# The attention of the first block: normalising before the transpose, the value product with V as weights, and a tail of 128 rows

## The reference, cut to what matters

```python
logits = jnp.einsum('bthd,btkhd->bthk', q_b, k_sel).astype(jnp.float32) * (HEAD_DIM ** -0.5)
logits = jnp.where(valid[:, :, None, :], logits, -jnp.inf)
p = jax.nn.softmax(logits, axis=-1).astype(v_sel.dtype)
return jnp.einsum('bthk,btkhd->bthd', p, v_sel)
```

## Time and profile before

| | |
|---|---|
| median of 3 runs | 1720.37 us (1720.04 to 1726.73) |
| the profiled execution | 1720.61 us |
| its span, first to last instruction | 1718.5 us |
| mean granted clock of TensorE | 0.979 |
| PE, DVE, ACT, POOL busy | 1640.2, 882.7, 384.0, 922.4 us |
| the stage `gates`, 322 to 534 us | PE busy 206.07 of 212 us |

### The profile page before, as it was taken

How to read it: one execution, slowest core, us unless ns; L and a number is a source line. 1 busy time by engine, 2 the same in 40 slices (tenths; PEclk the granted TensorE clock), 3 DMA queues, 4 the chain that set the end, 5 groups by cost and what they waited for, 6 DMA issues and landing times.

```text
span 1718.5 us, 23461 instructions
## 1 busy us (share of the span) xinstructions
PE 1640.2 (95%) x7899; PEld 1329.3 (77%) x7899; DVE 882.7 (51%) x1223; ACT 384.0 (22%) x740; POOL 922.4 (54%) x529
## 2 busy tenths in 40 slices
PE   4999999999999999999999998899788999999998
PEld 3769999877777888888888886677556788888886
DVE  6157830232443365531441456888655674574475
ACT  4130110123332012110110122143462330121122
POOL 4545555543446666757666665534213566666653
PEclk9999999999999999999999998899789999999998
DMA  4323333222122433333323332222001233333222
GB/s 154 90 74 86 87 81 90 76 61 57 54 61 83 143 98 90 94 98 97 87 85 110 88 96 67 68 62 62 25 25 50 86 98 93 91 98 98 88 84 86
DMA packets 264290, 142.61 MB, mean 83 GB/s; under 512 B 6205, under 2 KB 261461, under 8 KB 264101
## 3 DMA queue, kind: packets, MB, share of 16 engines
q1 hardware_dynamic: 262021, 139.26, 27.9%
q10 hardware_dynamic: 2208, 2.49, 0.4%
HBM read 137.41 MB, written 4.19 MB: 82 GB/s over the span
## 4 chain that ended last, share of the span: by engine, by line
PE 85%; DVE 10%; ACT 3%; issue 2%; DMA 0%; DVEq 0%; ACTq 0%; SPq 0%
PE PJ L548 64%; PE PJ L546 11%; PE PJ L871 1%; PE PB L702 1%; PE PX L683 1%; DVE CT L1416 1%; PE PB L693 1%; PE PX L636 1%; PE PB L703 1%; DVE H L1574 1%; DVE XC L1651 1%; DVE L L1609 0%; PE PJ L608 0%; DVE small L1596 0%; PE PX L857 0%
## 5 line engine op out<-in xcount | busy, mean ns | idle before, releaser
L494 POOL TENSOR_SCALAR WH<-RAW 128x1024 fp32r<-128x1024 f32 (+1 forms) x257 | 290.6, 1131 | 749.8 <-DMA RAW<-in_w_in_dram 325.5
L496 POOL TENSOR_TENSOR WL<-RAW,WH 128x1024 fp32r<-128x1024 f32 (+1 forms) x257 | 630.4, 2453 | 21.4
L548 PE MATMUL PJ<-AH,WH 128*128 128x512 f32 x944 | 381.0, 404 | 5.8 <-issue 3.4
L548 PE MATMUL PJ<-AH,WL 128*128 128x512 f32 x944 | 373.6, 396 | 0.0
L548 PE MATMUL PJ<-AL,WH 128*128 128x512 f32 x944 | 372.4, 395 | 0.0
L548 PE MATMUL PJ<-BH,WH 128*128 128x512 f32 x752 | 304.3, 405 | 7.3 <-DVE BL L1544 6.4
L548 PE MATMUL PJ<-BH,WL 128*128 128x512 f32 x752 | 299.9, 399 | 0.0
L548 PE MATMUL PJ<-BL,WH 128*128 128x512 f32 x752 | 299.6, 398 | 0.1
L548 PEld LDWEIGHTS PJ<-AH,WH 128*128 128x128 f32 x944 | 177.8, 188 | 54.5 <-issue 10.2
L548 PEld LDWEIGHTS PJ<-AL,WH 128*128 128x128 f32 x944 | 177.8, 188 | 40.8
L548 PEld LDWEIGHTS PJ<-AH,WL 128*128 128x128 f32 x944 | 177.8, 188 | 40.5 <-issue 0.2
(11 more groups left out here) (305 smaller groups left out, 1792.8 us busy)
## 6 DMA issues: line engine op xcount, KB each, us to landing
RAW<-in_w_in_dram SPq DMA_DIRECT2D x89, 512.0 KB, 3.7
RAW<-in_w_ff_up_dram SPq DMA_DIRECT2D x44, 512.0 KB, 3.8
RAW<-in_w_gate_dram SPq DMA_DIRECT2D x22, 512.0 KB, 3.8
RAW<-in_w_up_dram SPq DMA_DIRECT2D x22, 512.0 KB, 3.8
RAW<-in_w_out_dram SPq DMA_DIRECT2D x16, 512.0 KB, 3.9
RAW<-in_w_down_dram SPq DMA_DIRECT2D x16, 512.0 KB, 4.1
RAW<-in_w_ff_down_dram SPq DMA_DIRECT2D x16, 512.0 KB, 4.1
RAW<-in_w_conv_out_dram SPq DMA_DIRECT2D x8, 512.0 KB, 4.1
```

The costliest lines, as they stand in the source:

```text
L494: nc.gpsimd.tensor_scalar(WH[:, slot, 0:kc], RAW[:, slot, 0:kc], 1.0, 1.0, ALU.mult, ALU.mult).then_inc(w_hi, 1)
L496: nc.gpsimd.tensor_tensor(WL[:, slot, 0:kc], RAW[:, slot, 0:kc], WH[:, slot, 0:kc].bitcast(F32), ALU.subtract).then_inc(w_ready, 1)
L548: last = mm(bank_of(name, i)[0:rows], w[:, w_at, k, 0:rows], a[:, k, :], start=st, stop=sp_)
```

## The change

Three things are changed, all in the attention of `gates`:

1. The probabilities are scaled by the reciprocal of their row before they are transposed. The scaling is a DVE instruction on LT in place (144 to 528 columns), right behind the reciprocal; PE's `turn_p` waits for it (`p_scaled`) in place of `exp_done`. The scaling of the value product into YS is gone.
2. In `pv` V is the stationary operand and PT moves. The result then has the head width on the partitions, as QT wants it: `turn_y`, its wait and the YS tile are gone, and ACT copies PB7 into QT one step earlier (it waits for `pv_done`).
3. The tail product has 128 rows: the rows behind the 16 are set to zero once, in V by POOL near the start and in PT by DVE ahead of the stage. Two waits of ACT for these are new.

PE's loop of two rounds is written out, so that its waits are on constants.

```diff
+            pool.memset(V[:, QB, :], 0.0).then_inc(v_padded, 1)
@@ PE
-                pe.wait_ge(exp_done, i * (2 * NU) + (r * NU + u + 1))
+                pe.wait_ge(p_scaled, g + 1)
...
-                for t in range(b + 1):
-                    mm(PB7[:, 0:P], PT[:, u % 2, t * P:(t + 1) * P], V[:, t, at], start=t == 0, stop=False)
-                mm(PB7[:, 0:P], PT[0:META, u % 2, 4 * P:5 * P], V[0:META, b + 1, at],
-                   start=False, stop=True).then_inc(pv_done, 1)
-
-            def turn_y(i, r, u):
-                pe.wait_ge(ys_ready, i * (2 * NU) + (r * NU + u + 2))
-                pe.wait_ge(y_ready, i * (2 * NU) + (r * NU + u + 1))
-                nc.tensor.transpose(TURNED_Y[:, 0:P], YS[:, u % 2], ident[:]).then_inc(y_turned, 1)
+                pe.wait_ge(pt_ready, g + 2)
+                pe.wait_ge(y_ready, g + 1)
+                for t in range(b + 2):
+                    at = t if t <= b else QB
+                    last = mm(PB7[:, 0:P], V[:, t, h * P:(h + 1) * P], PT[:, g % 2, at * P:(at + 1) * P], start=t == 0, stop=t == b + 1)
+                last.then_inc(pv_done, 1)
...
-            with pe.Fori(0, 2) as i:
-                for r in range(2):
-                    for half in range(12):
+            for half in range(2 * COUNT["gates"]):
...
@@ ACT
+            act.wait_ge(v_padded, 1)
+            act.wait_ge(p_padded, 1)
-                    if 0 <= s - 3 < NU:
-                        u = s - 3
-                        act.wait_ge(y_turned, i * NU + (u + 1))
+                    if 0 <= s - 2 < NU:
+                        u = s - 2
+                        act.wait_ge(pv_done, i * NU + (u + 1))
...
-                           TURNED_Y[:, 0:P], ACT.Copy).then_inc(y_ready, 1)
+                           PB7[:, 0:P], ACT.Copy).then_inc(y_ready, 1)
@@ DVE
+            nc.vector.memset(PT[:, :, QB * P:(QB + 1) * P], 0.0).then_inc(p_padded, 1)
...
                         nc.vector.reciprocal(RINV[:, u % 4:u % 4 + 1], RS[:, u % 2:u % 2 + 1]).then_inc(rinv_ready, 1)
-                    if 0 <= s - 2 < NU:
-                        u = s - 2
                         dve.wait_ge(rinv_ready, i * NU + (u + 1))
-                        dve.wait_ge(pv_done, i * NU + (u + 1))
-                        ts(YS[:, u % 2], PB7[:, 0:P], RINV[:, u % 4:u % 4 + 1], None, ALU.mult).then_inc(ys_ready, 1)
+                        p = LT[:, u % 2, 0:EXT[units[u][1]]]
+                        ts(p, p, RINV[:, u % 4:u % 4 + 1], None, ALU.mult).then_inc(p_scaled, 1)
```

More of the change, by code:

```diff
@@ L238, in two_blocks @@
         QS = place(rt3, "QS", [P, 2, P])
-        YS = place(rt3, "YS", [P, 2, P])
         rt4 = again(r_t, t0)
@@ L676, in _, with qk @@
             NU = len(units)
[L678 to L683, removed]
+            def qk(g):
+                h, b = g // QB, g % QB
+                pe.wait_ge(qs_ready, g + 1)
+                pe.wait_ge(logits_ready, g + 1)
+                last = mm(PX[:, 0, 0:min(EXT[b], BANK)], QS[:, g % 2], KT[:, h, 0:min(EXT[b], BANK)], start=True, stop=True)
@@ L684, in qk, with turn_p @@
                 if EXT[b] > BANK:
-                    last = mm(PX[:, 1, 0:EXT[b] - BANK], QS[:, u % 2], head[:, BANK:EXT[b]], start=True, stop=True)
+                    last = mm(PX[:, 1, 0:EXT[b] - BANK], QS[:, g % 2], KT[:, h, BANK:EXT[b]], start=True, stop=True)
                 last.then_inc(qk_done, 1)
-            def turn_p(i, r, u):
-                j, b = units[u]
-                pe.wait_ge(exp_done, i * (2 * NU) + (r * NU + u + 1))
-                pe.wait_ge(pt_ready, i * (2 * NU) + (r * NU + u + 1))
+            def turn_p(g):
+                b = g % QB
+                pe.wait_ge(p_scaled, g + 1)
+                pe.wait_ge(pt_ready, g + 1)
@@ new lines, in _ @@
+            base = LETGO["gates"]
+            for half in range(2 * COUNT["gates"]):
+                j, turn, step_ = half // 2, half // 12, half % 12
+                if half % 2 == 0:
+                    i = 2 * (j // 6)
+                    if j % 3 == 2:
+                        pe.wait_ge(freed["dve"], base["dve"] + j // 3 + 1)
+                    else:
+                        pe.wait_ge(freed["act"], 2 * i + (base["act"] + (0, 0, None, 1, 2)[j % 6] - (1 if j % 6 == 0 else 0)))
+                panel("gates", j, j, a_x, mix, ks=halves()[half % 2], owner="here")
+                if 0 <= step_ - 2 < NU:
+                    pv(turn * NU + step_ - 2)
+                if 0 <= step_ - 1 < NU:
+                    turn_p(turn * NU + step_ - 1)
+                if step_ < NU:
+                    qk(turn * NU + step_)
@@ L1263, in _ @@
             ts, tt, stt = nc.vector.tensor_scalar, nc.vector.tensor_tensor, nc.vector.scalar_tensor_tensor
-            for e, credit in ((freed["dve"], CREDIT), (logits_ready, 1), (ys_ready, 1)):
+            for e, credit in ((freed["dve"], CREDIT), (logits_ready, 1)):
                 dve.sem_inc(e, credit)
```

16 lines of the change are left out of this document (7 added, 9 removed).

## The result

| | before | after |
|---|---|---|
| median of the runs | 1720.26 us (1720.04 to 1726.73, 4 runs) | 1753.14 us (1743.39 to 1754.93, 4 runs) |
| profiled execution, its span | 1720.61, 1718.5 us | 1754.61, 1752.9 us |
| first attention stage ends at | 533.78 us | 563.78 us |

Slower: ratio 1.017, 95% interval 1.0125 to 1.0215. The last row of the table is a mark that I use from here on: the start of the matmul behind the one wait of 2.10 us that closes the stage in every kernel. Up to it nothing but the stage differs. Here it is before and after, in PE's timelines.

A forecast was written before the change was run, and what follows sets the result against it. PE was taken as the bound, busy 95% of the span. Per turn, -3.2 us of list and the stops gave +5.3, with the clock +8.3; four turns +33 on 1720.6 us gave 1754 us, range 1738 to 1765.

The forecast's parts named there:

- What leaves PE: PE's list loses the transposes of results (0.9 us a turn) and tail time (2.3): -3.2 us a turn.
- Unit 0: PE at `turn_p` waits for the scaling, queued on DVE behind convolution and multiply into U: a stop of 3.9 us.
- Unit 5: PE at `turn_p` waits for the scaling, held by POOL's second pass after the second convolution: a stop of 3.65 us.
- the pass ends 7.27 after T4: POOL's pass at unit 5 ends 0.4 us later, from 6.87, counted from the start of unit 4's `turn_p` (T4).
- Unit 6: Reciprocal stands behind the multiply of step 7; PE at `turn_p` stops 0.8 us.
- Unit 7: POOL's second pass just ahead of the scaling: a stop of 1.6 us or 0; half taken, 0.8 us.
- Unit 1: Scaling waits for POOL's pass; a stop of 0.2 us in place of 0.9, so -0.7 us a turn.
- The stops together: Stop terms of a turn at PE's `turn_p`: +3.9 - 0.7 + 3.65 + 0.8 + 0.8 us.
- The clock: Two stops of over 3.5 us a turn each bring a clock fall of 1.6 us: 3.0 us a turn, bounds 0 and 3.2.
- Rival A: The stops come but the clock stays: 1742 us; chance 0.22.
- Rival B: POOL's passes don't meet the waits on DVE in steps 0, 5 and 8: -1.25 us a turn, 1715.6 us; chance 0.06.
- Rival C: The rows of the tail don't matter, all else as forecast: 1763 us; chance 0.07.

The follow-up runs named there:

- e6_order_tail16: e1_order with the last pass of each value product taking 16 rows again in place of 128: 1718.96 us.
- e1_order: Changed kernel, DVE reordered: convolutions at the end of the turn before, reciprocal and scaling ahead of the multiply into U: 1709.24 us.
- e9_before_order: Kernel before, with DVE's order of e1_order and no scaling to move: 1716.57 us.
- e10_recip_only: Changed kernel with only reciprocal and scaling moved ahead of the multiply into U, convolutions where they were: 1741.65 us.
- e3_pool_small: Changed kernel with POOL's passes over the weights of panels 48 to 67 cut from 1024 columns to 128: 1723.36 us.
- e2_fill: Changed kernel with unused products put on PE ahead of its waits of units 0 and 5: 1744.65 us.
- e5_before_padded: Kernel before, with its tail alone padded from 16 rows to 128: 1713.49 us.
- e4_order_act: e1_order with the scaling done by ACT behind its exponential in place of DVE: 1702.89 us.
- e8_act_scale: Changed kernel in its own order, with the scaling alone moved from DVE to ACT: 1737.61 us.
- e7_conv_only: Changed kernel with only the convolutions moved to the end of the turn before, reciprocal and scaling where they were: 1724.99 us.

## Why the prediction was right

The forecast was 1754 us, the median is 1753.14. Its own terms, one by one:

- **What leaves PE, -12.8 us in four turns: right, a little small.** The tail was to give 9.3 and gives 10.9, with the 0.06 us of the transposes behind it (e6_order_tail16 against e1_order). Those of the results were to give 3.5 and give 3.7 (e9_before_order against e6_order_tail16). Together -14.6 us. But each of the stops takes a little more than its idle time, which had no term: without the stops, a turn of after is still 0.8 us longer than one of e1_order (16.04 us against 15.81 from unit 7 to the next unit 0, and 0.2 us each at units 5, 6 and 7).
- **Unit 0, 3.9 us:** measured 3.38, 3.82, 3.83 and 3.81. e10_recip_only shows the multiply's part (0.65), e3_pool_small what is left with short passes (1.5).
- **Unit 5, 3.65 us:** measured 2.90 to 3.03. The mechanism held, the term was 0.7 too large. The step that failed is "the pass ends 7.27 after T4": the pass did not move. It starts 4.16 us after T4 (415.57 less 411.41), where it started 4.17 after it in the kernel before. The traces show why. The load of the weights did shift by the 0.4 us: SP issues it 1.16 us ahead of T4 before and 0.77 after. But the weights land 0.1 us sooner, and POOL's pass over the high part, which takes 1.35 us before, takes 1.05 after:

```profile
400.13 0.38 SPq L405 DMA_DIRECT2D RAW<-in_w_in_dram  x1
...
404.03 1.35 POOL L494 TENSOR_SCALAR WH<-RAW 128x1024 fp32r<-128x1024 f32 x1 [7.01 <-DMA RAW<-in_w_in_dram]
```

```profile
410.64 0.38 SPq L405 DMA_DIRECT2D RAW<-in_w_in_dram  x1
...
414.43 1.05 POOL L496 TENSOR_SCALAR WH<-RAW 128x1024 fp32r<-128x1024 f32 x1 [5.95 <-DMA RAW<-in_w_in_dram]
```

And DVE is through 0.16 us behind the pass's end, not 0.35.
- **Unit 6, 0.8:** 0.74 in every turn. **Unit 7, 1.6 in half of the turns:** 0.93 to 0.96 in all four, 3.8 us against the forecast's 3.2 (free, the scaling of 528 columns takes 0.69 us, not the 0.49 that I worked out). The prediction moved this pass 0.4 nearer to T6 with the same argument by which it moved the one of unit 5 away from T4, although both loads are issued ahead of their T; that the pass comes 3.65 to 3.70 after T6 in every turn has another reason, the stop of unit 6, by which T6 itself is later. **Unit 1, 0.2:** none. In the second turn the scaling meets the pass (1.04 us at 394.25 in place of 0.36) and is through at 395.29; PE would come to unit 1 at 395.5 even at the full clock (391.52 + 3.97), and in the same turn of e2_fill, where the clock is 1.00, it does not stop there either.
- **The stops together:** 30.3 us more than before, where the forecast had 33.8 (8.45 a turn: 3.9, -0.7, 3.65, 0.8 and 0.8).
- **The clock, two falls of 1.6 us a turn, 12 us in all:** seven falls in place of eight, at 1.7 each, 11.7 us. In size the term was right; that one of the eight would stay out, it could not tell. Rival A (no falls, 1742 us) was wrong for the profiled execution; e2_fill, which makes its condition true, gives 1744.65.

Stops and clock add 30.3 + 11.7 us, the list takes away 14.6; that leaves 2.6 of the stage's 30.0 us for what the stops cost beside their idle time, and the 0.8 us a turn above, 3 in all, agree with it. The other 4.4 us of span lie behind it, inside the 6.7 us by which that part wanders in kernels that leave it alone. So the stage came out 3 us under my 33 (the stops 3.5 less than forecast, 0.7 of it in unit 5 four times; the clock 0.3 less; list and restarts 0.8 more), and the rest of the program added about as much: that the median lies within 1 us of the forecast is partly chance.

Rival B (POOL's passes don't meet these waits) would have asked for scalings of 0.3 to 0.5 us; they took over 2 in units 5 and 7, and shortening the passes gave 30 us back. Rival C (rows of the tail cost nothing) fell with e5_before_padded and e6_order_tail16.

Left open: why one of the four runs of after took 1743.39 us. Its mean clock was 0.979 beside 0.972 to 0.974 in the others, so fewer falls would explain it; there is no trace of it.

## What to carry to other kernels

Before work is put between a producer and the busy engine, look at what the engine that will do it has ahead of that work in its queue: here the same instructions gave 44 us more or less by their place alone, and with the new order the kernel is 12 to 18 us faster than before (e1_order, e4_order_act), of which the order alone gives some 3 (e9_before_order). On this kernel a DVE instruction that another engine waits for should not share its moment with a POOL pass; move it, move the pass, or give it to ACT. And a part of a change that helps (here the padding of the tail, 6.5 us alone) is worth running by itself.

## What was unexpected of the hardware

- A tail of 16 rows among passes of 128 is dearer than one of 128: 0.28 to 0.29 us for its two passes, in both orders of the operands, and 0.06 more in the transposes behind them. Into the tail and out of it the first weight load starts together with its matmul, not 0.11 us before it as between passes of 128 rows.
- The clock does not always fall behind a stop of about 3 us: behind 2.94 us in the second turn of after it stayed at 1.00, behind 2.90, 2.91 and 3.03 in the other turns it fell, behind 1.4 us in e8_act_scale it stayed, behind 1.9 in e7_conv_only it fell twice and stayed once. Near the wait of 2.10 us that closes the stage (from 4 us ahead of the mark to 10 behind it) it fell in ten kernels and stayed in two.
- Time behind the stage differs by 6.7 us between kernels that are the same there, more than several of the effects studied.
